# The end of a layer: second token half by token rows, and the first half's scale one gate earlier

## The reference, cut to what matters

```python
def rms_norm(x, g):
    y = xf * lax.rsqrt(jnp.mean(xf * xf, axis=-1, keepdims=True) + EPS)
    return y * g
...
        x = x + rms_norm(f, g_ffn_post[i])
        e = jax.nn.sigmoid(x @ w_ple_gate[i]) * (p[i].astype(x.dtype) @ w_ple_proj[i])
        x = x + rms_norm(e, g_ple_post[i])
    return x
```

## Time and profile before

| | us |
|---|---|
| median of 3 runs (2745.42 to 2748.67) | 2745.88 |
| the profiled execution's own time | 2739.36 |
| its span | 2737.2 |
| TensorE busy, share of the span | 2586.7, 95% |
| VectorE busy | 1448.4, 53% |
| GpSimd busy | 1052.1, 38% |
| ScalarE busy | 532.7, 19% |
| mean granted TensorE clock | 0.975 |

### The profile page before, as it was taken

One profiled execution on the slowest core, in us unless ns is written; L12 is line 12 of the kernel. 1 busy time (PEld: TensorE's weight loads), 2 busy tenths in 40 slices (PEclk: granted clock), 3 DMA queues, 4 the chain that ended last, 5 costly groups with the idle time before them and its releaser, 6 DMA issues. The chain is left out here.

```text
span 2737.2 us, 29514 instructions
## 1 busy us (share of the span) xinstructions
PE 2586.7 (95%) x12016; PEld 2117.9 (77%) x12016; DVE 1448.4 (53%) x1183; ACT 532.7 (19%) x540; POOL 1052.1 (38%) x549
## 2 busy tenths in 40 slices
PE   6999999799989999989998799999999999999995
PEld 5888888577768888868876588888888888888774
DVE  4779776123665656741426744444444444444755
ACT  4100111345412323230013200000000000000432
POOL 2334332344535555523454433333333333333361
PEclk8999999899999999999998999999999999999997
DMA  5322222577866675653232211111111111111231
GB/s 197 105 95 85 100 92 86 188 235 247 276 176 185 182 212 150 172 169 138 92 138 93 93 46 47 47 46 46 55 52 46 46 46 46 46 46 61 93 108 62
DMA packets 276942, 304.06 MB, mean 111 GB/s; under 512 B 43821, under 2 KB 241786, under 8 KB 272762
## 3 DMA queue, kind: packets, MB, share of 16 engines
q1 hardware_dynamic: 246122, 248.88, 29.3%
q10 hardware_dynamic: 30736, 54.01, 5.4%
HBM read 216.35 MB, written 86.51 MB: 111 GB/s over the span
## 5 line engine op out<-in xcount | busy, mean ns | idle before, releaser
L436 PE MATMUL ps<-act_hi,w_hi 128*128 128x512 f32 x2288 | 912.3, 399 | 31.4 <-POOL w_lo L423 18.8
L440 PE MATMUL ps<-act_hi,w_lo 128*128 128x512 f32 x2288 | 906.2, 396 | 0.0
L439 PE MATMUL ps<-act_lo,w_hi 128*128 128x512 f32 x2288 | 901.7, 394 | 0.0
L421 POOL TENSOR_SCALAR w_hi<-w_raw 128x1024 fp32r<-128x1024 f32 x219 | 247.3, 1129 | 1412.5 <-PE ps L436 605.3
L423 POOL TENSOR_TENSOR w_lo<-w_raw,w_hi 128x1024 fp32r<-128x1024 f32 x219 | 575.1, 2626 | 18.3
L436 PEld LDWEIGHTS ps<-act_hi,w_hi 128*128 128x128 f32 x2288 | 433.8, 190 | 133.0 <-issue 24.2
L439 PEld LDWEIGHTS ps<-act_lo,w_hi 128*128 128x128 f32 x2288 | 433.8, 190 | 100.2 <-issue 3.6
L440 PEld LDWEIGHTS ps<-act_hi,w_lo 128*128 128x128 f32 x2288 | 433.8, 190 | 90.6
L2013 DVE TENSOR_TENSOR tile<-ps,tile 128x1024 f32<-128x1024 f32 x112 | 135.6, 1221 | 108.0 <-PE ps L1574 106.5
L2451 DVE SCALAR_TENSOR_TENSOR ring_a<-xin,par,ring_a 128x1024 f32<-128x1024 f32 x108 | 183.2, 1696 | 11.8 <-DVE ring_a L2445 0.3
L1574 PE MATMUL ps<-f_hi,w_lo 128*128 128x512 f32 x480 | 189.1, 394 | 0.0
(11 more groups left out here) (287 smaller groups left out, 2886.1 us busy)
## 6 DMA issues: line engine op xcount, KB each, us to landing
w_raw<-in_w_in_dram SPq DMA_DIRECT2D x34, 1024.0 KB, 5.4
spill<-ring_b ACTq DMA_DIRECT2D x67, 512.0 KB, 2.7
w_raw<-in_w_ffn_gate_dram SPq DMA_DIRECT2D x17, 1024.0 KB, 5.4
w_raw<-in_w_ffn_up_dram SPq DMA_DIRECT2D x17, 1024.0 KB, 5.4
w_raw<-in_w_ffn_down_dram SPq DMA_DIRECT2D x16, 1024.0 KB, 4.8
qkv_a<-spill SPq DMA_DIRECT2D x8, 1536.0 KB, 6.9
dec_a<-cum_rows SPq DMA_DIRECT2D x16, 512.0 KB, 12.5
gdn_in<-hrow SPq DMA_DIRECT2D x8, 1024.0 KB, 14.6
```

The source lines that it names most:

```text
L421: nc.gpsimd.tensor_scalar(hi, raw, 1.0, 0.0, ALU.mult, ALU.add).then_inc(split_done, 1)
L436: first = nc.tensor.matmul(o, wh, mov[0][:, k, c], start=(k == 0), stop=False)
L439: nc.tensor.matmul(o, wh, mov[1][:, k, c], start=False, stop=False)
L440: last = nc.tensor.matmul(o, wl, mov[0][:, k, c], start=False, stop=(k == KD - 1))
```

## The change

- In the first half, VectorE runs `scale_add` behind gate (1, 0) instead of behind gate (1, 1).
- In the second half ScalarE makes no squares of e, VectorE adds none, and there is no `lone_sum`, `factor`, `scale_add` or copy into a stage. Instead TensorE transposes e of the four token blocks into PSUM (`O_ET`) after the last gate; VectorE multiplies each block by the gain, which now lies along the row (a broadcast of `g_ple_post` in `fa[:, 1, :]`), into `e_all` in SBUF; ScalarE squares the same PSUM block with a sum over the row, after VectorE has read it; TensorE transposes x2 into the same PSUM buffers (`O_X2T`); VectorE makes the four factors per partition on 128x4 numbers, with ScalarE's root between; and one VectorE step per block, e·g·rs + x2 with x2 from PSUM, writes the result, which SP stores from `e_all`.
- SP's queue gets the load of `g_ple_post` (512 KB) behind the last weight block and ahead of the stores.
- Four small tiles of 128x4 are added near the start of SBUF. `e_all` takes the place of `act_lo3`, of whose columns it uses the first half's.
- The factor's steps become functions that the kernel's start uses too (the same instructions).

```diff
+    e_ss, e_ms, e_inv, e_rs = (sb(n, [P, 4]) for n in ("e_ss", "e_ms", "e_inv", "e_rs"))
...
+    sub = ExitStack()
+    e_all = sb("e_all", [P, KD, SEQ], f32, sub)
+    sub.close()
     act_lo3 = sb("act_lo3", [P, KD, SEQ], f32r, ph3)
...
+    def token_mean_by_dve(dve, stats, c, squares, n):
+
+        ss, ms, inv, rs = stats
+        dve.wait_ge(x_sq, squares)
+        nc.vector.tensor_scalar(ms[:, c], ss[:, c], 1.0 / D_MODEL, EPS, ALU.mult, ALU.add).then_inc(x_mean, 1)
+        dve.wait_ge(x_mean, n + 1)
+        nc.vector.reciprocal(inv[:, c], ms[:, c]).then_inc(x_mean, 1)
+
+    def token_refine_by_dve(dve, stats, c, factors, n):
+
+        ss, ms, inv, rs = stats
+        dve.wait_ge(x_fac, factors)
+        nc.vector.tensor_tensor(inv[:, c], rs[:, c], rs[:, c], ALU.mult).then_inc(x_mean, 1)
+        dve.wait_ge(x_mean, n + 1)
+        nc.vector.tensor_tensor(inv[:, c], inv[:, c], ms[:, c], ALU.mult).then_inc(x_mean, 1)
+        dve.wait_ge(x_mean, n + 2)
+        nc.vector.tensor_scalar(inv[:, c], inv[:, c], -0.5, 1.5, ALU.mult, ALU.add).then_inc(x_mean, 1)
+        dve.wait_ge(x_mean, n + 3)
+        nc.vector.tensor_tensor(rs[:, c], rs[:, c], inv[:, c], ALU.mult).then_inc(x_mean, 1)
+        dve.wait_ge(x_mean, n + 4)
...
-    O_N4 = [O_PG + 5, O_PG + 13]
-    O_OUT = [O_PG + i for i in (8, 9, 10, 11, 14, 15, 16, 17)]
+    O_N4 = O_PG + 5
+    O_OUT = [O_PG + i for i in (8, 9, 10, 11)]
+    O_ET = [O_PG + 14 + i for i in range(4)]
+    O_X2T = [O_PG + 18 + i for i in range(4)]
+    O_NONE = O_PG + 13
...
+    def e_rows(t):
+
+        return e_all[:, 2 * t:2 * t + 2, 0:HALF]
...
-        for t in range(NCH):
+        sp.wait_ge(x2_step, 24)
+        sp.dma_start(fa[:, 1, :], g_ple_post.broadcast_to([P, D_MODEL])).then_inc(grow_in, 16)
+        for t in range(4):
             b, c = uses(O_OUT[t], 0)
             sp.wait_ge(tile_free[b], c + 1)
             sp.dma_start(out_rows[t], out_st[:, t % 2, :]).then_inc(out_kept[t % 2], 16)
+        for t in range(4, NCH):
+            sp.wait_ge(fin_step, 12 + t - 3)
+            sp.dma_start(by_two(out_rows[t]), e_rows(t - 4)).then_inc(out_kept[t % 2], 16)
...
         pg_pair(1, 1)
         pg_pair(1, 2)
-        out_transposes(0)
+        pe.wait_ge(fin_step, 12)
+        for t in range(4):
+            rows_of(pj, O_OUT[t], t)
         pg_pair(1, 3)
-        lone_sum(O_N4[1], "n4", 1)
-        out_transposes(1)
+        b = uses(O_NONE, 0)[0]
+        wait_buffer(pe, O_NONE)
+        pe.sem_inc(tile_done[b], 1)
+        pe.wait_ge(e_done, 8)
+        for t in range(4):
+            rows_of(pj, O_ET[t], 4 + t)
+        for t in range(4):
+            rows_of(tile3, O_X2T[t], 4 + t)
...
-            act.wait_ge(e_done, i + 1)
-            square("n4", h, m, pair_of(pj, h, m))
+            if h == 0:
+                act.wait_ge(e_done, i + 1)
+                square("n4", h, m, pair_of(pj, h, m))
...
-        factor("n4", 1, O_N4[1])
-        out_copy(4)
-        out_copy(6)
+        b = uses(O_NONE, 0)[0]
+        act.wait_ge(tile_done[b], uses(O_NONE, 0)[1] + 1)
+        act.sem_inc(tile_free[b], 1)
+        a(e_rs[:, :], ones[:, 0:4], ACT.Sqrt).then_inc(x_fac, 1)
+        for t in range(4):
+            b = wait_tile(act, O_ET[t])
+            act.wait_ge(e_done, 8 + t + 1)
+            if t >= 2:
+                act.wait_ge(x_sq, NCH + t - 1)
+            a(ring3[:, t % 2, :], buf(b), ACT.Square, accum_out=e_ss[:, t:t + 1]).then_inc(x_sq, 1)
+        for t in range(4):
+            b = uses(O_ET[t], 0)[0]
+            act.wait_ge(x_sq, NCH + t + 1)
+            act.sem_inc(tile_free[b], 1)
+        act.wait_ge(x_mean, 12 + 2)
+        act.wait_ge(x_fac, 3)
+        a(e_rs[:, :], e_inv[:, :], ACT.Sqrt).then_inc(x_fac, 1)
...
-            if m >= 1:
+            if h == 0 and m >= 1:
                 square_sum("n4", h, m)
...
         e_gate(1, 0)
+        scale_add(pj, "g_ple_post", "n4", 0, fin_step, fin_add)
         e_gate(1, 1)
-        scale_add(pj, "g_ple_post", "n4", 0, fin_step, fin_add)
         e_gate(1, 2)
         out_copy(1)
         out_copy(3)
         e_gate(1, 3)
-        scale_add(pj, "g_ple_post", "n4", 1, fin_step, fin_add)
-        out_copy(5)
-        out_copy(7)
+        dve.wait_ge(grow_in, 32)
+        for t in range(4):
+            b = wait_tile(dve, O_ET[t])
+            v.tensor_tensor(e_rows(t), by_two(buf(b)), by_two(fa[:, 1, :]), ALU.mult).then_inc(e_done, 1)
+        token_factor_by_dve(dve, (e_ss, e_ms, e_inv, e_rs), slice(0, 4), NCH + 4, 12, 4)
+        for t in range(4):
+            b = wait_tile(dve, O_X2T[t])
+            v.scalar_tensor_tensor(out=e_rows(t), in0=e_rows(t), scalar=e_rs[:, t:t + 1], in1=by_two(buf(b)),
+                                   op0=ALU.mult, op1=ALU.add).then_inc(fin_step, 1)
```

More of the change, by code:

```diff
@@ L450, in pe_unit, with token_factor_by_dve @@
         return b
+    def token_mean_by_dve(dve, stats, c, squares, n):
[15 more added lines that the diff above has]
+        dve.wait_ge(x_mean, n + 4)
+    def token_factor_by_dve(dve, stats, c, squares, n, factors):
+        token_mean_by_dve(dve, stats, c, squares, n)
+        token_refine_by_dve(dve, stats, c, factors, n + 2)
     HEAD_SP, HEAD_L, TM_SRC, TM_END = 14, 15, 2, 3
@@ L1396, in hybrid_block_kernel @@
                ("n2", 1, 0), ("n2", 1, 1), ("n2", 1, 2), ("n2", 1, 3)] + \
-        [(name, h, m) for name in ("n3", "n4") for h in range(2) for m in range(4)]
+        [("n3", h, m) for h in range(2) for m in range(4)] + [("n4", 0, m) for m in range(4)]
     ADDED = [s for s in SQUARES if s[2]]
-    RS_COUNT = {("n1", 0): 1, ("n2", 0): 2, ("n1", 1): 3, ("n2", 1): 4, ("n3", 0): 5, ("n3", 1): 6, ("n4", 0): 7, ("n4", 1): 8}
+    RS_COUNT = {("n1", 0): 1, ("n2", 0): 2, ("n1", 1): 3, ("n2", 1): 4, ("n3", 0): 5, ("n3", 1): 6, ("n4", 0): 7}
     STEP = {"S0": 1, "S1": 2, "S2": 3, "S3": 4, "A0": 5, "S4": 6, "S5": 7, "A1": 8, "S6": 9, "S7": 10, "A2": 11, "A3": 12}
@@ L1685, in pg_pair, with rows_of @@
             last.then_inc(tile_done[b], 1)
-        def out_transposes(h):
-            pe.wait_ge(fin_step, 12 * (h + 1))
-            for t in range(4 * h, 4 * h + 4):
-                b = wait_buffer(pe, O_OUT[t])
-                for k in range(KD):
-                    last = nc.tensor.transpose(buf(b)[:, k * P:(k + 1) * P], pj[:, k, t * P:(t + 1) * P], ident[:, :])
-                last.then_inc(tile_done[b], 1)
+        def rows_of(src, o, t):
+            b = wait_buffer(pe, o)
+            for k in range(KD):
+                last = nc.tensor.transpose(buf(b)[:, k * P:(k + 1) * P], src[:, k, t * P:(t + 1) * P], ident[:, :])
+            last.then_inc(tile_done[b], 1)
         for m in range(4):
@@ L1697, in pe_tail @@
         pg_pair(1, 0)
-        lone_sum(O_N4[0], "n4", 0)
+        lone_sum(O_N4, "n4", 0)
         pg_pair(1, 1)
         pg_pair(1, 2)
-        out_transposes(0)
+        pe.wait_ge(fin_step, 12)
+        for t in range(4):
+            rows_of(pj, O_OUT[t], t)
         pg_pair(1, 3)
-        lone_sum(O_N4[1], "n4", 1)
-        out_transposes(1)
+        b = uses(O_NONE, 0)[0]
[6 more added lines that the diff above has]
+            rows_of(tile3, O_X2T[t], 4 + t)
     def act_tail(act):
@@ L1862, in act_tail @@
         pg_out(1, 0)
-        factor("n4", 0, O_N4[0])
+        factor("n4", 0, O_N4)
         pg_out(1, 1)
@@ L2370, in token_mean @@
         def token_mean(i):
-            c = slice(4 * i, 4 * i + 4)
-            dve.wait_ge(x_sq, 4 * i + 4)
-            v.tensor_scalar(x_ms[:, c], x_ss[:, c], 1.0 / D_MODEL, EPS, ALU.mult, ALU.add).then_inc(x_mean, 1)
-            dve.wait_ge(x_mean, 6 * i + 1)
-            v.reciprocal(x_inv[:, c], x_ms[:, c]).then_inc(x_mean, 1)
-        def token_refine(i):
-            c, n = slice(4 * i, 4 * i + 4), 6 * i + 2
-            dve.wait_ge(x_fac, i + 1)
-            v.tensor_tensor(x_inv[:, c], x_rs[:, c], x_rs[:, c], ALU.mult).then_inc(x_mean, 1)
-            dve.wait_ge(x_mean, n + 1)
-            v.tensor_tensor(x_inv[:, c], x_inv[:, c], x_ms[:, c], ALU.mult).then_inc(x_mean, 1)
-            dve.wait_ge(x_mean, n + 2)
-            v.tensor_scalar(x_inv[:, c], x_inv[:, c], -0.5, 1.5, ALU.mult, ALU.add).then_inc(x_mean, 1)
-            dve.wait_ge(x_mean, n + 3)
-            v.tensor_tensor(x_rs[:, c], x_rs[:, c], x_inv[:, c], ALU.mult).then_inc(x_mean, 1)
-            dve.wait_ge(x_mean, n + 4)
+            token_mean_by_dve(dve, (x_ss, x_ms, x_inv, x_rs), slice(4 * i, 4 * i + 4), 4 * i + 4, 6 * i)
+        def token_refine(i):
+            token_refine_by_dve(dve, (x_ss, x_ms, x_inv, x_rs), slice(4 * i, 4 * i + 4), i + 1, 6 * i + 2)
         def token_h(t):
```

## The result

| | before | after |
|---|---|---|
| median, us (15 runs each, same chip) | 2744.74 | 2754.07 |
| lowest to highest | 2737.51 to 2749.46 | 2749.53 to 2758.55 |
| profiled execution, its own time | 2739.36 | 2758.28 |
| its span | 2737.2 | 2756.6 |

The ratio after to before is 1.0035 (95% interval 1.0025 to 1.0045): slower by 0.35%, where 0.85% faster was forecast, and far outside the range. The steps that the prediction costed at the end of the layer came close to the forecast. The time was lost in the 2600 us ahead of it, in TensorE's products.

What follows compares the result with a forecast made beforehand. TensorE, busy 95% of the span, was taken as the bound, with two gaps at the layer's end. Savings of 8.3 + 1.85 + 13.4 = 23.5 us off the median 2745.88 gave 2722.4 us, range 2718.5 to 2728.5.

Steps and rivals of the forecast that it cites:

- Parts 1 and 2: First half's end: earlier scale cuts TensorE's gap from 9.1 to 0.8 (8.3 us); output transposes at full clock save 1.85 us.
- One term put at nothing: Splits beside the first half's scale: GpSimd loses 0.3 us per split, but no weight is late, so nothing.
- Part 3: Second half's end: the row-wise path from last product to end takes 19.6 us against 33.0, saving 13.4 us.
- the upper bound of 4.1: Last final step to end of span: 3.1 us, plus 0.3 for the stores' faster arrival, with bounds 0 to 1.
- A: Transposes of e after the last gate: clock falls before or during the gate, 1 to 2 us more, 2723.9; chance 0.12.
- B: First half's scale: splits block VectorE longer, TensorE waits 4 to 6 us and its clock falls, 2728; chance 0.09.
- C: Second half's row-wise end: squares wait for multiplies without overlap, x2 transposes behind them, 5 us more, 2727.5; chance 0.08.
- D: All matmuls: four tiles move others by 64 bytes; 2.0 ns each cancels the gain; chance 0.02 slower, 0.03 within 0.2%.

Runs made afterwards that it cites:

- unshifted: Changed kernel with its four small tiles declared at the end of SBUF, so no other tile moves; 2718.4 against 2739.47 for before, ratio 0.9921.
- the tiles first: Changed kernel with its four small tiles declared ahead of the weights' tiles, so both operands move by 128 bytes; 2717.0 against 2739.99 for before, ratio 0.9913.
- both operands moved: Kernel before with an unused 128-byte tile ahead of all tiles, so weights and moving tiles both move; 2735.29 against 2739.47, ratio 0.9989.
- the rows alone: Unshifted kernel with the first half's scale behind gate (1, 1) as before, so only the row-wise end is new; 2727.25 against 2745.48 for before, ratio 0.9934.
- without low parts: Unshifted kernel with GpSimd writing zeros, by a one-input instruction, as low part of the last five units' weights; one run of 2726.17.
- the scale's place alone: Kernel before with only the first half's scale moved ahead of gate (1, 1); 2736.18 against 2745.48, ratio 0.9969.

## Why the prediction was wrong

| step | forecast | unshifted | after |
|---|---|---|---|
| gap ahead of the output transposes, us | 0.8 | 0.67 | 0 |
| scale of the first half, us | 19.3 | 19.5 | 17.1 |
| 32 transposes, us | 3.9 | 3.71 | 3.66 |
| last product's end to the end, us | 19.6 | 20.0 | 20.05 |
| spacing of the products in the reduced format, ns | 229.0 (as before) | 229 | 233.3 |
| ratio to before | 0.9914 | 0.9921 | 1.0035 |

**Parts 1 and 2 were right** within 0.2 us for the unshifted kernel, by their own mechanisms. One term put at nothing wasn't: the split beside the scale ends late, and in the unshifted kernel the 96 products of pairs (1, 1) and (1, 2) take 22.8 us instead of 22.5. In the kernel after, the gap is zero for reasons that weren't foreseen. The scale takes 17.1 and not 19.5, since the third split falls mostly on gate (1, 1) behind it (3.42 us instead of 1.2). And from its start to the end of `pg_pair(1, 2)` it is 19.6 instead of 18.9 us, with slower products and a wait of 0.37 for GpSimd.

**Part 3 was right in its sum**, with two terms off that nearly cancel, which is luck. The four squares come at 1.13 (1.28 forecast from the kernel's start), 0.6 less. From the last final step's end to the end of the span it is 4.25 (2704.25 to 2708.5) instead of 3.4, 0.85 more, and just above the upper bound of 4.1. The prediction took the landing time of one 2048 KB transfer for the four stores and found nearly nothing. In the trace the DMA engines can't keep up with them. Final steps with x2 from PSUM took 4.85 (4.9), multiplies 4.62 for four. Slips of 0.05 us in its sums (the scale alone is 9.93, not 9.96) change nothing.

**Rivals.** A is true but small: about 1 us, in three of six profiled kernels. The prediction reasoned that after 2.4 us of idle the clock should still be up, since it had fallen 3.1 and 3.0 us after TensorE's work stopped. But the fall isn't at a fixed time after that: before's own trace has a third one 4.5 us behind the last product (mean clock 0.88 in 2708 to 2709), and in the three kernels with A it came 2.2, 3.0 and 3.7 us behind the last product, in two of them when TensorE was already transposing. That the clock stayed up in the kernel after was luck; 0.12 for A was too low. What decides it is open. B and C weren't seen: the splits cost what was forecast, and the squares overlapped the multiplies.

**D decided, and the failed step is its "against".** The prediction named the mechanism, that the four tiles move nearly all others and that a few ns in each product would eat the gain, with the threshold of 2.0 ns, and then set it at 0.02 with two sentences. "No row shows that an address matters" was no evidence: before has one set of addresses, so none of its rows could show it. "Both operands of a product move alike" was false. The weight tiles are declared ahead of the four, so they stay, and only the moving data shift. That could be read in the code. The shift is also 128 bytes, not 64, as each tile takes 32 bytes per partition. Measured, the cost is 4.3 ns per product. With the prediction's own line from 2.0 ns (gain gone) to 3 ns (2758) that gives a loss. Its 12,016 matmuls were too many: only the 9552 in the reduced format pay, the transposes don't.

Before's own trace had a hint that was passed over. In L1570, L1573 and L1574 (480 products each, 1603 to 2547 us, clock 1.0) it is 225.8, 229.2 and 231.7 ns from one start to the next. So the spacing isn't fixed by the column count and the clock. The prediction took 0.23 us for all. Nor does it belong to the kind of product: in the unshifted kernel, with the same addresses, the same three take 231.7, 225.8 and 229.2. Only their mean stays.

**What it comes to.** The change at the layer's end is worth 21 us (unshifted, interval 13 to 30; with the tiles first, 24 us, 18 to 30), against 23.5 forecast. The shift costs 33 us as run alone (21 to 44) and 40 in the trace. Together 9 us were lost, which by the medians leaves 30 to 33 for the shift. The 40 compares two single executions, of which before's was 5.4 under its median and after's 4.2 over.

## What to carry to other kernels

A tile declared between two operands' tiles moves one against the other, and a change of 4 ns in each of some 9500 products outweighs all that is won at the end of a layer; so work out every operand's start before and after a change, put small new tiles ahead of both or behind both, and try the distance that the runs found best. When a price per instruction is unknown and the count is in the thousands, the absence of a row is no argument: give such a rival the chance that one can't exclude it, and take the code's order of declarations as evidence. A step moved beside GpSimd's splits can be costed from an earlier place where the same two run side by side: here this came within 0.2 us in the unshifted kernel, and 2 us too high in the kernel after, where the splits began at other moments.

## What the runs showed of the hardware

- Products of 512 columns in the reduced format follow each other at 226.7 ns if the start of the moving operand and that of the weights are equal modulo 256 bytes, 229.0 at 64 apart, 232.5 at 128, 233.3 at 192 or at an odd multiple of 32; at 8 and 16 apart 233.2 and 231.7. Bfloat16 (215.8) and float32 (429.2 per pass) don't depend on it. Why is open: no run shows what is read together, nor why 256 columns turn the order round.
- At distance 64 the pace isn't fixed. In the kernel with both operands moved, in that with the new tiles first (1388 to 1435 us), in that with the rows alone (`pg_pair(1, 3)`) and in that without low parts (2634 to 2665 us) some stretches ran at 233.3 with the starts of the fast ones. In before, in the unshifted kernel and in that with the scale's place alone there was none. Each was seen in one profiled execution. What picks the pace is open, and it may be part of the spread of before (2731.7 to 2760.4 over 17 runs on one chip).
- At distance 64 three products in turn take 225.8, 229.2 and 231.7 ns, and which of the three kinds takes which changes from kernel to kernel at the same addresses. At distance 0 all take 226.6 to 226.8 (the same three lines), at 192 all 233.3 to 233.4.
- TensorE's granted clock fell from 1.0 to 0.5 at 2.2, 3.0 and 3.7 us behind the last product in three kernels, around the same wait of 2.43 us, and stayed at 1.0 in three others.
- Four stores of 512 KB in pieces of 2 KB, 1.19 us apart, kept the DMA engines at a share of 1.02 and 381 GB/s, and the span ended 4.25 us behind the last step that fed them.
- Up to the scale's start the unshifted kernel was 5.6 us ahead of the forecast (2654.2 against 2659.8), though nothing before it differs from before. That is in the spread of single executions, and a reason to read steps from trace to trace but gains from many runs.
- VectorE's steps of two SBUF inputs lost 3.2 us for each split with a subtraction (3.25 us long, of two inputs), and about 1 us for each split whose instructions both have one input (the second 1.37 us long).
